# Moving the token sums, the first block sums' loads and the last tiles' roots in a one-core hybrid mixer layer

## The chip, the core and the metric

The kernel runs on one core of one Trainium2 chip. The metric is the device time of one execution in microseconds (us). "Span" is the time from the first to the last instruction of the one execution that the profiler recorded.

## What is computed

One layer: a normalised input goes through one projection, two head groups work on it (a gated recurrence and a gated convolution), and their concatenated result `mixed` (512 tokens x 2048) goes through the output projection, a root-mean-square norm and a residual addition. The part that the change touches is the end:

```python
mixed = jnp.concatenate([o_a, o_b], axis=-1)              # (1, 512, 2048)
y = jnp.einsum('btm,md->btd', mixed, w_out[l])            # 512 x 2048 by 2048 x 2048
x = x + y * lax.rsqrt(jnp.mean(y * y, axis=-1, keepdims=True) + EPS) * post_norm_g
```

## The kernel before, in words

All weights stream through a ring of `RING = 4` slots. A unit is 128 x 1024 of float32: SyncE (SP) loads it into `w_raw`; ScalarE (ACT) rounds it into `w_hi`; the rest `w_lo = w_raw - w_hi` is made by GpSimd (POOL, `lo_unit`, L430) for all units up to the first two of the last stage, and by VectorE (DVE, `fast_rest`, L1241) after that. TensorE (PE) multiplies each unit in three products (hi by hi, hi by lo, lo by hi), 24 matmuls of 128 x 512 for a full unit, 12 for a unit of the fast kinds.

The 2048 output columns are done in four chunks of 512. **Chunk 0** is a plain product, the loop over `s` in `range(OUT_U)` (8 units; `out_products`). In the same loop every engine still carries the last head (head 7) along: `slot(H-1, s)` on PE, `late(H-1, s)` on ACT and DVE, and the last convolution tile `ln_tile(J-1, ...)`. Unit `s` on PE waits for `mlo_done, 2s + 2`: rows `2s` and `2s+1` of `h_lo`, made by DVE in `mix_lo(at)` (L1177) from what ACT rounded in `mix_hi(at)` (L724). `mix_lo(12)` and `(13)` stand in DVE's step 5, `(14)` in step 6, `(15)` in step 7. The last of them needs head 7's result: PE's `slot(7, 6)`, ACT's logarithm and exponential (L684, L686), DVE's L1145 and L1148, then `mix_hi(15)`.

**Chunks 1 to 3** are done by `STEPS`, a list written out by hand: P1 x4, C 0, P2 x4, P5 x4, P6 0, 1, C 1, P6 2, 3, P7 ..., P3 ..., P4 ..., and C 5 to 7 last. C steps are plain products for chunk 1 (24 matmuls). The P steps get a 2 x 2 block product out of seven block products; they need sums of weights (`bsum`, `sum_weights`) and sums of tokens (`sum_sides(n, at)`, L1200: `n` 0 to 3 for the four sums, `at` 0 to 2 for their parts, 128 x 1024, 128 x 512, 128 x 512, in place in `mix`). P5 reads sum 1, P6 sum 2, P7 sum 0, P3 sum 3. ACT's `side_rounded` waits for them (`m_summed`), DVE's `side_rest` (L1232) follows.

SP's queue: units `s` of chunk 0 through L312, and behind each of units 4 to 7 one load of a `bsum` block (L384), 512 KB each. The first of these waits for `lev_done, 4 * H` (head 7's scores are done, since `bsum` lies in the same memory) and `qdec_ready, H`. Then the units of `LOADS` follow, each when its slot is free.

At the end PE does C 5 to 7 token tile by token tile (`tt` 0 to 3) and signals `y_mm` after each. ACT squares each tile from PSUM (L733), and only after the four squares does it take the roots, tile by tile: logarithm (L827), exponential (L829). DVE per tile: the sum of the tile's four partial sums (L1322), the product with the gain (`take_y`, L1181), four multiply-adds with the residual (L1328). SP stores the tile (L404), the last one in four pieces.

```python
for tt in range(TT):                      # DVE, the end
    dve.wait_ge(y_sq, TT * (CHUNKS - 1) + tt + 1)
    V.tensor_reduce(rst[:, TT + tt:TT + tt + 1], ssq[:, tt * CHUNKS:(tt + 1) * CHUNKS], AX.X, ALU.add).then_inc(y_ssum, 1)
    take_y(1, tt, y1[:, tt * 512:(tt + 1) * 512], bank(tt))
    dve.wait_ge(y_rs, 2 * (tt + 1))
```

Of the kernel before, what the change touches and what calls it, by code (L numbers as in the profile page):

```python
# [27 lines left out]
def build_layer(nc, x, pre_norm_g, post_norm_g, w_in, lb_logits, hg_norm_g, dw_kernel, dw_bias,  # L28
                conv_ln_g, conv_ln_b, w_out, out):
    fp32, fp32r, i8 = mybir.dt.float32, mybir.dt.float32r, mybir.dt.int8  # L30
    ALU, ACT, AX = mybir.AluOpType, mybir.ActivationFunctionType, mybir.AxisListType
    ds = bass.ds
    P = 128
    _, T, D = x.shape
# [3 lines left out]
    H = W_A // P  # L38
# [3 lines left out]
    TT = T // P  # L42
    UW = HK * P
    RING = 4
    EPS, LB_FLOOR = 1e-6, 1e-30
# [10 lines left out]
    CHUNKS = D // 512  # L56
    OUT_U = (W_A + W_B) // (2 * P)
    N_FAST = N_OUT + OUT_U
    HU = OUT_U // 2
# [33 lines left out]
    SIDE = {step: i for i, step in enumerate([step for step in STEPS if step[0] in ("P5", "P6", "P7", "P3")])}  # L93
    SIDES = 3
    SUM_PARTS = ((0, 4), (4, 2), (6, 2))
    SUM_ORDER = [(0, 0), (0, 1), (0, 2), (1, 0), (2, 0), (3, 0), (1, 1), (2, 1), (3, 1), (1, 2), (2, 2), (3, 2)]
    M_SUM = {done: at + 1 for at, done in enumerate(SUM_ORDER)}
    JOINED = {"c11": 2, "u2": 4, "u4": 5, "c22": 7, "u3": 9, "c12": 11, "c21": 13}
    SUM_OF = {"P7": 0, "P5": 1, "P6": 2, "P3": 3}
# [33 lines left out]
    with ctx:  # L133
# [175 lines left out]
        @block.sync  # L309
        def _(sp):  # L310
            def load_unit(n, slot, src, width):
                sp.dma_start(w_raw[:, slot * UW:(slot + 1) * UW].rearrange("p (k c) -> p k c", c=width),  # L312
                             src.rearrange("(k p) c -> p k c", p=P)).then_inc(raw_in[slot], 16)

            def in_unit(n, slot, half, col):
                load_unit(n, slot, w_in[0, half * UW:(half + 1) * UW, ds(col, P)], P)

            def first_loads():

                for at, n in enumerate(FIRST):  # L320
                    in_unit(n, n, n % 2, CONV_COLS[n // 2])
                    if at >= 2:
                        x_load(at)
                par_loads()

            def conv_loads(j):
                for s in range(CONV_U):
                    n = CONV_U * j + s
                    if n < RING:
                        continue  # L330
                    sp.wait_ge(raw_in[n % RING], 16 * (n // RING))
                    sp.wait_ge(lo_done, FIRST.index(n - RING) + 1 if n < 2 * RING else n - RING + 1)
                    if s < 4:
                        in_unit(n, n % RING, s % 2, CONV_COLS[s // 2] + j * P)
                    else:
                        k = VK * (2 * (j % VH) + s - 4)
                        load_unit(n, n % RING, w_in[0, k * P:(k + VK) * P, ds(COL_V + j // VH * VW, VW)], VW)

            def x_load(tt):
                if tt < 2:  # L340
                    for half in range(2):
                        a, b = half * UW, (half + 1) * UW
                        sp.dma_start(mix[:, tt * D + a:tt * D + b], x[0, tt * P:(tt + 1) * P, a:b]).then_inc(x_in[2 * tt + half], 16)
                else:
                    sp.dma_start(mix[:, tt * D:(tt + 1) * D], x[0, tt * P:(tt + 1) * P, :]).then_inc(x_in[2 + tt], 16)

            def par_loads():

                dwr = dw_kernel[0].rearrange("w (j c) -> (w j) c", c=P)
                R1 = TAPS * J - P  # L350
                sp.dma_start(stage[:, 0:P], dwr[0:P, :]).then_inc(par_in, 16)
                sp.dma_start(stage[0:R1, P:2 * P], dwr[P:TAPS * J, :]).then_inc(par_in, 16)
                sp.dma_start(stage[R1:R1 + J, P:2 * P], dw_bias[0].rearrange("(j c) -> j c", c=P)).then_inc(par_in, 16)
                for n, v in enumerate((conv_ln_g, conv_ln_b, lb_logits)):
                    sp.dma_start(stage[n * J:(n + 1) * J, 2 * P:3 * P], v[0].rearrange("(j c) -> j c", c=P)).then_inc(par_in, 16)
                sp.dma_start(stage[3 * J:3 * J + 1, 2 * P:3 * P], hg_norm_g).then_inc(par_in, 16)

            x_load(0)
            x_load(1)
            first_loads()  # L360
            for j in range(J):
                conv_loads(j)
            with sp.Fori(0, H) as h:
                for u in range(HEAD_U):
                    n = N_HEAD + HEAD_U * h + u
                    cut_before = held(sp, n - RING + 1)
                    sp.wait_ge(raw_in[u % RING], 16)
                    sp.wait_ge(lo_done, cut_before)
                    in_unit(n, u % RING, u % 2, HEAD_COLS[u // 2] + h * P)
            def out_rows(s):  # L370

                return slice(2 * P * PAIRS[s], 2 * P * (PAIRS[s] + 1))

            for s in range(OUT_U):
                n = N_OUT + s
                sp.wait_ge(raw_in[s % RING], 16 * (n // RING))
                sp.wait_ge(lo_done, n - RING + 1)
                load_unit(n, s % RING, w_out[0, out_rows(s), 0:512], 512)
                if s >= HU:
                    u = s - HU  # L380
                    if u == 0:
                        sp.wait_ge(lev_done, 4 * H)
                        sp.wait_ge(qdec_ready, H)
                    sp.dma_start(bsum[u].rearrange("p (k c) -> p k c", c=512),  # L384
                                 w_out[0, out_rows(u), ds(COL_2, 512)].rearrange("(k p) c -> p k c", p=P)).then_inc(first_in[u], 16)
            for q, step in enumerate(LOADS):
                n = N_FAST + q
                sp.wait_ge(raw_in[q % RING], 16 * (n // RING))
                if q < RING:
                    sp.wait_ge(lo_done, n - RING + 1)  # L390
                else:
                    used = LOADS[q - RING]
                    if used[0] in ("P1", "P6", "P4"):
                        sp.wait_ge(b_summed, SUMMED[used])
                    else:
                        sp.wait_ge(fast_lo, AT[used] - 1)
                s, col = load_of(step)
                load_unit(n, q % RING, w_out[0, out_rows(s), ds(col, 512)], 512)
            parts = 0
            for tt in range(TT):  # L400
                for a, b in out_parts(tt):
                    parts += 1
                    sp.wait_ge(y_out, parts)
                    sp.dma_start(out[0, tt * P:(tt + 1) * P, a:b], mix[:, tt * D + a:tt * D + b]).then_inc(stored, 16)  # L404
            sp.wait_ge(stored, 16 * parts)
# [68 lines left out]
        def _(act):  # L474
# [253 lines left out]
            def square(c, tt, y):  # L728

                if squares[0]:  # L730
                    act.wait_ge(y_sq, squares[0])
                squares[0] += 1
                A(near[:, 0:512], y, ACT.Square, accum_out=ssq[:, tt * CHUNKS + c:tt * CHUNKS + c + 1]).then_inc(y_sq, 1)  # L733

            def out_hi(s):
                n = N_OUT + s + AHEAD
# [82 lines left out]
            act.wait_ge(joined, JOINED["c21"])  # L819
            for tt in (0, 1):  # L820
                square(2, 2 + tt, pair_c21[:, tt * 512:(tt + 1) * 512])
            for tt in range(TT):
                act.wait_ge(y_mm, TT - 1 + tt + 1)
                square(1, tt, bank(tt))
            for tt in range(TT):
                act.wait_ge(y_ssum, tt + 1)
                A(rst[:, tt:tt + 1], rst[:, TT + tt:TT + tt + 1], ACT.Ln, scale=1.0 / D, bias=EPSB).then_inc(y_rs, 1)  # L827
                act.wait_ge(y_rs, 2 * tt + 1)
                A(rst[:, tt:tt + 1], rst[:, tt:tt + 1], ACT.Exp, scale=-0.5).then_inc(y_rs, 1)  # L829


        @block.vector
        def _(dve):
# [428 lines left out]
            for s in range(OUT_U):  # L1262
# [5 lines left out]
                    ln_tile(J - 1, s - 2, False)  # L1268
                for at in {2: (6, 7), 3: (8, 9), 4: (10, 11), 5: (12, 13), 6: (14,), 7: (15,)}.get(s, ()):
                    mix_lo(at)  # L1270
                if s == 4:
                    for at in range(3):
                        sum_sides(0, at)
                    for n in (1, 2, 3):
                        sum_sides(n, 0)
                if s == 6:
                    for n in (1, 2, 3):
                        sum_sides(n, 1)
            for m, (kind, u) in enumerate(STEPS):
                if m + 1 < len(STEPS) and STEPS[m + 1][0] in AHEAD_SUM:  # L1280
                    sum_weights(*STEPS[m + 1])
# [8 lines left out]
                if (kind, u) == ("P1", 3):  # L1290
                    dve.wait_ge(gain_in, 32)
                    for tt in range(TT):
                        dve.wait_ge(y_mm, tt + 1) if tt < TT - 1 else dve.wait_ge(unit_done, N_FAST)
                        take_y(0, tt, y0[:, tt * 512:(tt + 1) * 512], bank(tt))
                if (kind, u) == ("P2", 0):
                    for n in (1, 2, 3):
                        sum_sides(n, 2)
                if (kind, u) == ("P5", 2):
                    dve.wait_ge(kept, 1)
                    join(("P2", 3), pair_c11, 6, pair_c11)  # L1300
# [15 lines left out]
            join(("P4", 3), pair_c21, 4, pair_c21, JOINED["u3"])  # L1316
            gain(3, pair_c12, TT + 6)
            gain(2, pair_c21, TT + 8)
            dve.wait_ge(res_in, 16 * TT)
            for tt in range(TT):  # L1320
                dve.wait_ge(y_sq, TT * (CHUNKS - 1) + tt + 1)
                V.tensor_reduce(rst[:, TT + tt:TT + tt + 1], ssq[:, tt * CHUNKS:(tt + 1) * CHUNKS], AX.X, ALU.add).then_inc(y_ssum, 1)  # L1322
                take_y(1, tt, y1[:, tt * 512:(tt + 1) * 512], bank(tt))
                dve.wait_ge(y_rs, 2 * (tt + 1))
                dve.wait_ge(y_taken, TT * (CHUNKS - 1) + tt + 1)
# [321 lines left out]
```

## Time and profile before

| | us |
|---|---|
| median of 3 runs | 891.15 |
| lowest | 889.8 |
| the profiled execution, whole | 890.06 |
| its span | 888.2 |
| PE busy in the span | 858.7 (97%) |
| DVE busy | 648.5 (73%) |
| ACT busy | 413.8 (47%) |

Of the three timed runs one took 1669.31 us; the other two lie within 0.2% of each other. The whole time of the profiled execution is 1.86 us more than its span. TensorE's clock is given as a share of full speed (1.00 is 2.4 GHz, 0.50 is 1.2 GHz).

### The profile page before, as it was taken

How to read it: one execution, taken by the hardware profiler on the slowest of the kernel's cores; microseconds unless marked ns; L12 is line 12 of the kernel's file. 1: busy time of each engine (PE TensorE's matmuls, PEld its weight loads, DVE VectorE, ACT ScalarE, POOL GpSimd, SP SyncE). 2: the span in 40 equal slices, each digit the busy share in tenths (PEclk: the TensorE clock that was granted, in tenths of full speed). 3: DMA queues.
4: the chain of work that ended last, by engine and by line, in shares of the span. 5: the costliest groups of instructions: out<-in, count | busy, mean ns of one | idle time of the engine just before them, and what ended most of it. 6: DMA issues, size and time to landing. Idle time of an engine off the chain costs nothing.

```text
span 888.2 us, 12341 instructions
## 1 busy us (share of the span) xinstructions
PE 858.7 (97%) x4210; PEld 720.1 (81%) x4210; DVE 648.5 (73%) x1029; ACT 413.8 (47%) x648; POOL 311.9 (35%) x143
## 2 busy tenths in 40 slices
PE   8999999999999999999999999999999988999991
PEld 7988888888888888888888888888888866888881
DVE  4687778778778984948667594957759977697745
ACT  7523323322222464756457475646647641654331
POOL 3284444435434354242525334242533350000000
PEclk9999999999999999999999999999999998999996
DMA  9253333333333323232413313241321082434824
GB/s 308 79 147 100 102 101 96 96 95 95 94 96 95 95 71 104 63 96 58 125 53 94 94 47 94 71 118 47 94 94 48 1 308 74 140 119 142 296 84 189
DMA packets 119165, 96.07 MB, mean 108 GB/s; under 512 B 2864, under 2 KB 101465, under 8 KB 117849
## 3 DMA queue, kind: packets, MB, share of 16 engines
q1 hardware_dynamic: 118377, 90.33, 33.2%
q10 hardware_dynamic: 752, 5.25, 1.4%
q8 instruction: 23, 0.38, 0.2%
q14 instruction: 13, 0.11, 0.0%
HBM read 91.38 MB, written 4.19 MB: 108 GB/s over the span
## 4 chain that ended last, share of the span: by engine, by line
PE 94%; DVE 3%; issue 1%; DMA 1%; ACT 0%; DVEq 0%; POOL 0%; SPq 0%; ACTq 0%; POOLq 0%
PE banks L1425 19%; PE banks L1427 19%; PE banks L1426 19%; PE banks L1440 3%; PE banks L1442 3%; PE banks L1441 3%; PE banks L1598 3%; PE banks L1599 3%; PE banks L1597 3%; PE banks L1562 3%; PE banks L1371 3%; PE banks L1563 3%; PE banks L1564 3%; DVE mix L1200 1%; PE banks L1473 1%; PE banks L1483 1%
## 5 line engine op out<-in xcount | busy, mean ns | idle before, releaser
L430 POOL TENSOR_TENSOR w_lo<-w_raw,w_hi 128x1024 fp32r<-128x1024 f32 x122 | 305.8, 2510 | 420.3 <-ACT w_hi L485 419.8
L1425 PE MATMUL banks<-h_hi,w_hi 128*128 128x512 f32 x736 | 291.1, 396 | 0.0
L1427 PE MATMUL banks<-h_hi,w_lo 128*128 128x512 f32 x736 | 286.7, 390 | 0.0
L1426 PE MATMUL banks<-h_lo,w_hi 128*128 128x512 f32 x736 | 286.5, 389 | 0.0
L485 ACT ACTIVATE w_hi<-w_raw 128x1024 fp32r<-128x1024 f32 x120 | 126.5, 1055 | 175.7 <-PE banks L1427 81.3
L900 DVE SCALAR_TENSOR_TENSOR banks<-work,tap,banks 128x512 f32<-128x512 f32 x232 | 175.3, 756 | 8.0
L1427 PEld LDWEIGHTS banks<-h_hi,w_lo 128*128 128x128 f32 x736 | 138.1, 188 | 29.3
L1426 PEld LDWEIGHTS banks<-h_lo,w_hi 128*128 128x128 f32 x736 | 138.3, 188 | 28.2 <-issue 0.5
L1425 PEld LDWEIGHTS banks<-h_hi,w_hi 128*128 128x128 f32 x736 | 138.3, 188 | 27.9 <-issue 0.5
L1562 PE MATMUL banks<-w_hi,h_hi 128*128 128x512 f32 x128 | 51.3, 400 | 7.4 <-DVE h_lo L1177 7.4
L1563 PE MATMUL banks<-w_lo,h_hi 128*128 128x512 f32 x128 | 50.4, 394 | 0.0
L1564 PE MATMUL banks<-w_hi,h_lo 128*128 128x512 f32 x128 | 50.3, 393 | 0.0
L1440 PE MATMUL banks<-w_hi,h_hi 128*128 128x512 f32 x128 | 49.8, 389 | 0.0
L1441 PE MATMUL banks<-w_lo,h_hi 128*128 128x512 f32 x128 | 49.8, 389 | 0.0
L1442 PE MATMUL banks<-w_hi,h_lo 128*128 128x512 f32 x128 | 49.8, 389 | 0.0
L1241 DVE TENSOR_TENSOR w_lo<-w_raw,w_hi 128x1024 fp32r<-128x1024 f32 x22 | 26.7, 1222 | 13.1 <-ACT w_hi L757 13.1
L1562 PEld LDWEIGHTS banks<-w_hi,h_hi 128*128 128x128 f32 x128 | 24.4, 191 | 13.2 <-issue 8.2
L757 ACT ACTIVATE w_hi<-w_raw 128x1024 fp32r<-128x1024 f32 x24 | 24.9, 1054 | 21.4 <-PE banks L1564 10.7
L1101 DVE COPY_PREDICATED work<-mask,banks 128x192 f32<-128x192 int8 (+2 forms) x48 | 14.5, 303 | 27.5 <-PE banks L1483 20.2
L922 DVE SCALAR_TENSOR_TENSOR work<-banks,work 128x512 f32<-128x512 f32 x8 | 5.5, 692 | 32.1 <-ACT work L493 32.1
L1086 DVE COPY_PREDICATED work<-mask,banks 128x256 f32<-128x256 int8 x16 | 11.9, 743 | 23.3 <-PE banks L1473 22.5
L1564 PEld LDWEIGHTS banks<-w_hi,h_lo 128*128 128x128 f32 x128 | 24.4, 191 | 5.3
(211 smaller groups left out, 1261.6 us busy)
## 6 DMA issues: line engine op xcount, KB each, us to landing
w_raw<-in_w_in SPq DMA_DIRECT2D x112, 512.0 KB, 3.7
w_raw<-in_w_out SPq DMA_DIRECT2D x40, 512.0 KB, 4.5
mix<-in_x ACTq DMA_DIRECT2D x4, 1024.0 KB, 11.9
out_y<-mix SPq DMA_DIRECT2D x3, 1024.0 KB, 3.9
mix<-in_x SPq DMA_DIRECT2D x4, 512.0 KB, 5.5
mix<-in_x SPq DMA_DIRECT2D x2, 1024.0 KB, 10.0
work<-in_w_out SPq DMA_DIRECT2D x4, 512.0 KB, 8.7
gates<-in_post_norm_g ACTq DMA_DIRECT2D x1, 1024.0 KB, 6.7
```

The source lines that it names most:

```text
L430: g.tensor_tensor(w_lo[:, a], w_raw[:, a], w_hi[:, a].bitcast(fp32), ALU.subtract).then_inc(lo_done, 1)
L485: A(w_hi[:, a], w_raw[:, a], ACT.Copy).then_inc(hi_done, 1)
L900: V.scalar_tensor_tensor(dst, src, tp[:, w:w + 1], acc, ALU.mult, ALU.add).then_inc(tap_done, 1)
L1425: mm(bank(b), wh, hh, start=kt == 0, stop=False)
L1426: mm(bank(b), wh, hl, start=False, stop=False)
L1427: ins = mm(bank(b), wl, hh, start=False, stop=kt == KT - 1)
L1440: mm(o, h_hi[:, a], w_hi[:, w], start=vu == 0 and k == 0, stop=False)
L1441: mm(o, h_hi[:, a], w_lo[:, w], start=False, stop=False)
L1442: ins = mm(o, h_lo[:, a], w_hi[:, w], start=False, stop=vu == 2 * VH - 1 and k == VK - 1)
L1562: mm(o, h_hi[:, a], w_hi[:, w], start=first and k == 0, stop=False)
L1563: mm(o, h_hi[:, a], w_lo[:, w], start=False, stop=False)
L1564: ins = mm(o, h_lo[:, a], w_hi[:, w], start=False, stop=last and k == 1)
```

## The change

Four edits. The order of the sums (`SUM_ORDER`) becomes sum by sum, and their calls leave DVE's loop over `s` (steps 4 and 6) for the loop over `STEPS`: sums 0 and 1 stand in P2 0 and P2 1, sum 2 in P2 3, sum 3 in P5 1. The four `bsum` loads leave SP's loop over `s`, and each now stands behind one of the first four loads of `LOADS`; the wait for head 7's scores stands behind the first of these. On ACT, the root of each last tile follows its own square. For that the three other chunks' partial sums are added by DVE ahead of the tiles and scaled (eight instructions on one column each), and the logarithm takes them as its bias.

```diff
-    SUM_ORDER = [(0, 0), (0, 1), (0, 2), (1, 0), (2, 0), (3, 0), (1, 1), (2, 1), (3, 1), (1, 2), (2, 2), (3, 2)]
+    SUM_ORDER = [(n, at) for n in range(4) for at in range(3)]
...
                 load_unit(n, s % RING, w_out[0, out_rows(s), 0:512], 512)
-                if s >= HU:
-                    u = s - HU
-                    if u == 0:
-                        sp.wait_ge(lev_done, 4 * H)
-                        sp.wait_ge(qdec_ready, H)
-                    sp.dma_start(bsum[u].rearrange("p (k c) -> p k c", c=512),
-                                 w_out[0, out_rows(u), ds(COL_2, 512)].rearrange("(k p) c -> p k c", p=P)).then_inc(first_in[u], 16)
...
                 load_unit(n, q % RING, w_out[0, out_rows(s), ds(col, 512)], 512)
+                if q == 0:
+                    sp.wait_ge(lev_done, 4 * H)
+                    sp.wait_ge(qdec_ready, H)
+                if q < HU:
+                    sp.dma_start(bsum[q].rearrange("p (k c) -> p k c", c=512),
+                                 w_out[0, out_rows(q), ds(COL_2, 512)].rearrange("(k p) c -> p k c", p=P)).then_inc(first_in[q], 16)
...
-                A(near[:, 0:512], y, ACT.Square, accum_out=ssq[:, tt * CHUNKS + c:tt * CHUNKS + c + 1]).then_inc(y_sq, 1)
+                A(near[:, 0:512], y, ACT.Square, accum_out=ssq[:, tt * CHUNKS + (c - 1) % CHUNKS:tt * CHUNKS + (c - 1) % CHUNKS + 1]).then_inc(y_sq, 1)
...
+            act.wait_ge(y_ssum, 2 * TT)
             for tt in range(TT):
                 act.wait_ge(y_mm, TT - 1 + tt + 1)
                 square(1, tt, bank(tt))
-            for tt in range(TT):
-                act.wait_ge(y_ssum, tt + 1)
-                A(rst[:, tt:tt + 1], rst[:, TT + tt:TT + tt + 1], ACT.Ln, scale=1.0 / D, bias=EPSB).then_inc(y_rs, 1)
+                act.wait_ge(y_sq, squares[0])
+                A(rst[:, tt:tt + 1], ssq[:, tt * CHUNKS:tt * CHUNKS + 1], ACT.Ln, scale=1.0 / D,
+                  bias=rst[:, TT + tt:TT + tt + 1]).then_inc(y_rs, 1)
                 act.wait_ge(y_rs, 2 * tt + 1)
                 A(rst[:, tt:tt + 1], rst[:, tt:tt + 1], ACT.Exp, scale=-0.5).then_inc(y_rs, 1)
...
-                if s == 4:
-                    for at in range(3):
-                        sum_sides(0, at)
-                    for n in (1, 2, 3):
-                        sum_sides(n, 0)
-                if s == 6:
-                    for n in (1, 2, 3):
-                        sum_sides(n, 1)
...
-                if (kind, u) == ("P2", 0):
-                    for n in (1, 2, 3):
-                        sum_sides(n, 2)
+                if kind == "P2" and u < 2:
+                    for at in range(3):
+                        sum_sides(u, at)
+                if kind == "P2" and u == 3:
+                    for at in range(3):
+                        sum_sides(2, at)
+                if (kind, u) == ("P5", 1):
+                    for at in range(3):
+                        sum_sides(3, at)
...
             gain(2, pair_c21, TT + 8)
+            for tt in range(TT):
+                a = slice(TT + tt, TT + tt + 1)
+                V.tensor_reduce(rst[:, a], ssq[:, tt * CHUNKS + 1:(tt + 1) * CHUNKS], AX.X, ALU.add).then_inc(y_ssum, 1)
+            dve.wait_ge(y_ssum, TT)
+            for tt in range(TT):
+                a = slice(TT + tt, TT + tt + 1)
+                V.tensor_scalar(rst[:, a], rst[:, a], 1.0 / D, EPS, ALU.mult, ALU.add).then_inc(y_ssum, 1)
             dve.wait_ge(res_in, 16 * TT)
             for tt in range(TT):
                 dve.wait_ge(y_sq, TT * (CHUNKS - 1) + tt + 1)
-                V.tensor_reduce(rst[:, TT + tt:TT + tt + 1], ssq[:, tt * CHUNKS:(tt + 1) * CHUNKS], AX.X, ALU.add).then_inc(y_ssum, 1)
                 take_y(1, tt, y1[:, tt * 512:(tt + 1) * 512], bank(tt))
```

## Rows read from the trace of the kernel before

**Rows 1.** The page, part 1: busy us (share of the span), instructions.

```profile
PE 858.7 (97%) x4210; PEld 720.1 (81%) x4210; DVE 648.5 (73%) x1029; ACT 413.8 (47%) x648; POOL 311.9 (35%) x143
```

**Rows 2.** Waits of PE from 690 us on: in total, times, longest.

```profile
PE banks L1562 <- DVE h_lo L1177: 7.4, 1, 7.4
```

**Rows 3.** Windows: stretch, length, busy us of each engine, PE's granted clock, DMA, GB/s.

```profile
729.70:733.00 3.30, 0.00 (x0) 0.00 (x0) 3.20 (x2) 1.46 (x3) 3.29 (x2) 1.00 0.42 158
737.00:740.40 3.40, 3.33 (x8) 2.69 (x9) 3.15 (x6) 0.00 (x0) 0.00 (x0) 0.50 0.00 0
...
749.60:760.50 10.90, 10.90 (x50) 9.01 (x49) 7.28 (x9) 6.67 (x12) 0.00 (x0) 1.00 0.29 93
760.50:777.00 16.50, 16.50 (x74) 13.69 (x73) 10.80 (x12) 8.69 (x10) 0.00 (x0) 1.00 0.51 159
```

**Rows 4.** Chain that ended last, around the pause: start, us, what.

```profile
710.59 5.15 DMA w_raw<-in_w_out
...
716.72 0.62 ACT work L602
717.37 2.48 DVE mix L980
...
739.97 0.43 PE banks L1562
...
740.91 0.23 PE banks L1562
```

**Rows 5.** Timeline of DVE: start, us, line, operation, tiles, idle before it.

```profile
711.45 0.73 DVE L1138 SCALAR_TENSOR_TENSOR work<-work,ebl,banks 128x128 f32<-128x128 f32 x2
...
720.97 14.74 DVE L1200 TENSOR_TENSOR mix<-mix 128x1024 f32<-128x1024 f32 x6
...
740.36 0.75 DVE L1148 SCALAR_TENSOR_TENSOR mix<-work,par 128x512 f32<-128x512 f32 x1
```

**Rows 6.** Timeline of ACT.

```profile
728.90 1.06 ACT L757 ACTIVATE w_hi<-w_raw 128x1024 fp32r<-128x1024 f32 x1 [1.19 <-PE banks L1564]
...
730.57 0.63 ACT L686 ACTIVATE work<-work 128x512 f32<-128x512 f32 x1
```

**Rows 7.** Timeline of POOL.

```profile
724.70 8.61 POOL L430 TENSOR_TENSOR w_lo<-w_raw,w_hi 128x1024 fp32r<-128x1024 f32 x3 [0.27 <-ACT w_hi L485]
```

**Rows 8.** Waits of SP's queue from 650 us on.

```profile
SPq L384 <- PE banks L1492: 22.0, 1, 22.0
```

**Rows 9.** Groups of DVE by form, 718 to 770 us: busy, mean ns, idle before.

```profile
L1200 DVE TENSOR_TENSOR mix<-mix 128x512 f32<-128x512 f32 x8 | 9.8, 1238 | 0.4
L1200 DVE TENSOR_TENSOR mix<-mix 128x1024 f32<-128x1024 f32 x4 | 9.0, 2251 | 0.2
L1241 DVE TENSOR_TENSOR w_lo<-w_raw,w_hi 128x1024 fp32r<-128x1024 f32 x7 | 8.4, 1223 | 8.5 <-ACT w_hi L757 8.5
...
L1177 DVE TENSOR_TENSOR h_lo<-mix,h_hi 128x512 fp32r<-128x512 f32 x6 | 3.9, 684 | 0.8 <-ACT h_hi L724 0.8
```

**Rows 10.** Timeline of ACT and DVE at the end.

```profile
865.46 0.60 ACT L733 ACTIVATE near<-banks 128x512 f32<-128x512 f32 x1 [3.39 <-PE banks L1564]
...
869.54 0.60 ACT L733 ACTIVATE near<-banks 128x512 f32<-128x512 f32 x1 [3.39 <-PE banks L1564]
...
870.13 0.28 ACT L827 ACTIVATE rst<-rst,epsb 128x1 f32<-128x1 f32 x1
870.44 0.20 ACT L829 ACTIVATE rst<-rst 128x1 f32<-128x1 f32 x1
870.68 0.75 DVE L1328 SCALAR_TENSOR_TENSOR mix<-gates,rst,mix 128x512 f32<-128x512 f32 x1 [11.83 <-ACT rst L829]
...
873.33 0.15 DVE L1322 TENSOR_REDUCE rst<-ssq 128x1 f32<-128x4 f32 x1
873.40 0.68 DVE L1181 TENSOR_TENSOR work<-banks,gates 128x512 f32<-128x512 f32 x1
...
881.87 2.07 DVE L1328 SCALAR_TENSOR_TENSOR mix<-work,rst,mix 128x512 f32<-128x512 f32 x3
```

## The prediction

> **What bounds the kernel now.** I read the page first, for the engine that holds the time: PE is busy in 97% of the span [rows 1]. So the question is where PE pauses and what stands behind its last matmul. From 690 us on, PE waits for another engine exactly once: 7.4 us in front of unit 6 of chunk 0 (L1562), for DVE's L1177, which is `mix_lo` [rows 2]. The windows put the pause at 729.7 to 737.1; at its end the granted clock is 0.50, the lower level of 1.2 GHz, and PE does 8 matmuls in 3.3 us there [rows 3]. The chain around the pause shows 0.43 us for one matmul in that stretch and 0.23 us once the clock is back [rows 4].
>
> Who is late? DVE's timeline has six token sums (L1200) from 720.97 to 735.71, and `mix_lo(12)` and `(13)` stand behind them in DVE's order [rows 5]. The chain shows the first cause: a load that lands at 715.7, then ACT's L602, then DVE's L980 [rows 4]. DVE's head work before it ended at 712.2 [rows 5]; it then had nothing to do until L602, which stood on ACT behind `out_hi(3)`, the rounding of unit 5. That unit's load stood in SP's queue behind the first `bsum` load, which waited 22.0 us for head 7's scores [rows 8]. So both moved parts of the change bear on this one pause.
>
> The end is the second place. The last matmul ends near 869.5; ACT squares tile 3 and only then takes the first root, so DVE, which could work on tile 0 much earlier, sat idle 11.83 us and does four tiles in a row from 870.68 to 883.94 [rows 10]. Output stores take the rest up to 888.2, 4.26 us.
>
> **Part 1: sums and loads moved, the pause.** Unit 5's load no longer waits, so ACT rounds it on time and L602 runs before 712 (DVE gave it its input before the row at 711.45 [rows 5]), L980 at 712.2, right behind DVE's head work. Even at L980's price in the chain, 2.48 us [rows 4], it ends at 714.7. `mix_lo(13)` needs `mix_hi(13)`, which stands on ACT behind the rounding of unit 7, which needs the slot of unit 3 (716 on PE: 729.7 less units 4 and 5 at 5.44 and 2.5 us of head work between them); two such steps at 1.06 [rows 6] and about 0.6 put `mix_lo(12)` to `(14)` at 721 at the latest, also when POOL disturbs them. PE wants them at 729.7. The 7.4 us go.
>
> What is late next is unit 7, which wants `mix_lo(15)` at 729.66 + 24 x 0.227 = 735.1. PE's `slot(7, 6)` ends at 729.7 as before; ACT rounds unit F1 at 728.90 and its exponential L686 ends at 731.20, both as before [rows 6]. Then DVE's L1145 and L1148 (0.68 by L1177's form [rows 9], 0.75 [rows 5]), ACT's `mix_hi(15)` (0.63, by L686's form) and `mix_lo(15)` (0.68) come to 734.2 with the hand-overs between them. In the kernel before DVE came to L1148 only at 740.36. The margin is 0.9 us.
>
> POOL is the doubt here: it makes F1's rest from about 730.0 on, and L1148 and `mix_lo(15)` have two SBUF inputs each. In the kernel before, POOL's three operations up to 733.3 took 8.61 us [rows 7], 2.87 each. The Trainium skill (SBUF — State Buffer, Who interferes with whom) says that a DVE operation with two SBUF inputs and a GpSimd operation that reads SBUF exclude each other for a whole instruction, and that other such pairs don't touch. By that rule L1148 would wait to 732.4 and the margin would be 0.5, not 0.9.
>
> Without a pause the clock has no reason in this trace to fall (it is 1.00 in the windows beside the pause [rows 3]): 8 matmuls at 0.23 are 1.8 us instead of 3.4, so 1.6 more. Part 1: 7.4 + 1.6 = **9.0 us**. From below it could be less by what `mix_lo(15)` is late: bounded by L980's excess, 2.48 - 0.68 = 1.8 us, less the margin, so a loss of 0.9.
>
> **Part 1, the other side: where the work goes.** All twelve sums are 9.8 + 9.0 = 18.8 us in the kernel before [rows 9], 4.7 for one group of three. An undisturbed operation of the same shape takes 1.22 (128 x 1024, L1241) and 0.68 (128 x 512, L1177) [rows 9]; a group is 2.6. The nearer row is the clean one: POOL's last operation ends at 733.3 [rows 7], and the first moved sum runs after 750. The rule above says the same; by the disturbed row a group would be 4.7. I take 2.6 and keep 4.7 as the upper end.
>
> Does DVE have the room? In 749.6 to 777.0 it is idle 3.6 + 5.7 = 9.3 us with one group of 2.3 us already there [rows 3]. Four groups are 10.4, so 8.1 more: tight. I walk it through, with all PE times 9.0 earlier (P1 0 at 740.6, a P step 2.72 us, a C step 5.44). C 0 starts at 751.5, P2 0 at 756.9, P2 1 at 759.6, P2 2 at 762.4, P2 3 at 765.1, P5 0 at 767.8, P5 1 at 770.5, P6 0 at 778.7. ACT rounds a step when the unit four before it is done. DVE: rest of C 0 until 750.3 (1.1 ahead, as the kernel before has it), of P2 0 until 751.5; sum 0 until 754.1; rest of P2 1 until 755.3; sum 1 until 757.9; rest of P2 2 until 759.1 (3.3 ahead); of P2 3 until 760.3; sum 2 until 762.9; P5 0's two rests until 764.8 (3.0 ahead); P5 1's until 766.7 (3.8 ahead); sum 3 until 769.3; P5 2 until 771.2 (2.0 ahead); the join of c11 and P6 0's weight sum until 773.7; P5 3 until 775.6 (0.3 to 0.4 ahead); P6 0 with the next weight sum until 778.7, just in time. The sums of 512 overlap a little (three took 2.28 in the kernel before), which gives some 0.25 a group, 1 us in all, as a cushion. I take **0**, with 0 to 2 us at the clean price. ACT's `side_rounded` for P5 0 waits for sum 1's first part at 756.5; behind it in ACT's queue is the rounding of P5 0, which can't start before 759.6 anyway.
>
> The loads: units 5 to 7 and F0 go 15 us and more earlier; the four `bsum` loads are issued from 710.1 on, as before, with F1 to F3 between them, each when POOL has freed a slot (the last near 720). In the kernel before these took up to 11 us to land, with everything issued at once; even so the last is there by 731, and its sum (P1 3) is wanted at 743. Cost 0. The other users of SP's queue stand behind what frees their slots, which moves with PE.
>
> **Part 2: the roots.** Added on DVE: four reductions and four scalings of one column, 0.15 each by L1322 [rows 10]; the scaling is not in the trace, bounded by 0.07 (the distance at which L1181 follows L1322) and 0.28 (ACT's one-column L827). That is 0.6 to 1.7 us once, in front of tile 0. New wait: ACT's first square waits for them, and behind it stand the other squares. Tile 0's matmuls end near 857.3 in the kernel before (869.5 less three tiles), and the gains ahead of the additions about then; so tile 0's square is 0.6 to 1.7 late. Tiles come every 4.08 us (869.54 - 865.46), and DVE needs 0.68 + 0.75 + 2.07 = 3.5 for one [rows 10], so the lateness is gone by tile 2. ACT per tile: 0.60 + 0.19 + 0.28 + 0.20, 1.3.
>
> So tiles 0 to 2 are finished while PE works on the next. What is left behind the last square (870.13 in the kernel before): logarithm and exponential until 870.65, beside them `take_y` until 870.9, then 0.75 + 2.07 until 873.75. The same point was 883.94. **10.2 us** go: three tiles of 3.5 less 0.3 for the product that now stands in the path. The stores of the last tile's pieces end 4.26 us later, as before; with the third tile's megabyte only a little further ahead of them, 0 +/- 0.5.
>
> **Sum.** 9.0 + 10.2 = 19.2 us. Profiled execution: 890.06 - 19.2 = 870.9. The median of the runs shown is 1.1 higher, which would give 872.0; the lowest is 0.3 lower. I say 871.
>
> **Rivals.**
> *A, DVE becomes the bound in P2 to P6.* At the disturbed price (4.7 a group) the same walk puts P2 2's rest at 763.5 against 762.4, P5 0's 2.4 and P5 2's 3 us late, P6 0's some 6 to 7. Against it: nothing runs on POOL then. For it: my margin at P6 0 is nil. Time: 871 + 6.5 = 877.5. A milder form, 1 to 3 us in short pauses (or `mix_lo(15)` late by 0.9), gives 872 to 874.
> *B, the change lifts only half.* Something else than the sums holds `mix_lo(12)` and `(13)`, so the pause stays near 7 us and only the end is gained: 890.06 - 10.2 = 879.9. Against it: each link of the chain [rows 4] is either moved or has its input by 712.
> *C, slower.* The clock. PE runs through from 690 to 860 without the one rest it had; if the granted clock fell to the 0.50 that [rows 3] show for as little as 97 matmuls (19.2 / 0.20), 42 us of work at that level, all is given back (890), and beyond that point the kernel is slower: 911 at 200 matmuls. Against it: in this trace the level of 0.50 follows a pause and never full work.
>
> **Chances.** Both parts in full, 869 to 872.5: 0.66. Milder A, 872.5 to 875: 0.17. A in full: 0.08. B: 0.04. C: 0.01. Better than forecast, since the stores or later steps gain too: 0.04. The range that holds 8 in 10 runs from 868.5 to 876. A measurement of this kernel tells some 2% from no change; that line lies at 873.3 (from 891.15), or 872.3 from the profiled execution, only 1.4 to 2.4 us above the forecast. Faster by over 2%: 0.70 of the cases lie under it, less 0.07 for that closeness, 0.63. Within 2%: 0.36. Slower: 0.01.
>
> **What the profile will show.** Right: no wait of PE from 690 us to its last matmul, clock 1.00 through 729 to 745, first P1 matmul near 740.6; twelve L1200 after 750 at 1.2 and 0.7 us; the last matmul near 860.5; ACT alternating square, logarithm, exponential every 4.08 us; 7.9 us from the end of the last square to the end of the span, where it was 18.1. Wrong: PE waiting for L1241 or L1232 in P5 or P6 steps (A); PE waiting for L1177 near 729 or 735 (B, or POOL's port); DVE waiting for a `bsum` load; clock 0.50 anywhere in the stage (C).

## The result, and the profile after

The changed kernel takes 870.25 us (median of four runs, 869.83 to 870.59); the kernel before takes 890.71 beside it (median of four). The ratio is 0.9773, with a 95% interval of 0.9754 to 0.9793. One of these four, 1669.31 us, fell out of line: the ratio leaves it out, and the median of the other three is 890.27. The span is 868.4 us instead of 888.2, 19.8 less; I had forecast 19.2. The changed kernel's line numbers differ a little: `mix_lo` is L1176 (was L1177), the sums L1199 (L1200), the rests L1240 (L1241), the last multiply-adds L1331 (L1328), the matmuls of chunk 0 L1565 to L1567.

The page of the changed kernel, part 1, against [rows 1]:

```profile
PE 857.1 (99%) x4210; PEld 719.2 (83%) x4210; DVE 645.6 (74%) x1033; ACT 413.4 (48%) x648; POOL 311.2 (36%) x143
```

PE's work is the same to within 2 us, its share went from 97% to 99%: what was saved was PE's idle time. PE waits for no other engine between 690 us and its last matmul, where [rows 2] had 7.4 us. The windows of the changed kernel over the old pause, to be held against the first two of [rows 3]:

```profile
729.70:733.00 3.30, 3.30 (x16) 2.67 (x15) 1.50 (x2) 1.70 (x3) 2.42 (x1) 1.00 0.00 0
733.00:740.40 7.40, 7.40 (x34) 6.15 (x33) 5.47 (x6) 1.69 (x2) 0.00 (x0) 1.00 0.39 120
```

PE is busy for all of both, 34 matmuls stand where there were 8 in the last 3.4 us, and the clock is 1.00. DVE's timeline of the changed kernel shows the head's last work, against [rows 5]:

```profile
709.75 5.68 DVE L1176 TENSOR_TENSOR h_lo<-mix,h_hi 128x512 fp32r<-128x512 f32 x2
...
716.72 0.69 DVE L979 TENSOR_TENSOR mix<-work 128x512 f32<-128x512 f32 x1
717.32 5.30 DVE L1176 TENSOR_TENSOR h_lo<-mix,h_hi 128x512 fp32r<-128x512 f32 x5
731.47 0.69 DVE L1144 TENSOR_TENSOR work<-banks,work 128x512 f32<-128x512 f32 x1 [8.85 <-ACT work L685]
732.20 1.04 DVE L1147 SCALAR_TENSOR_TENSOR mix<-work,par 128x512 f32<-128x512 f32 x1
734.00 0.69 DVE L1176 TENSOR_TENSOR h_lo<-mix,h_hi 128x512 fp32r<-128x512 f32 x1 [0.76 <-ACT h_hi L723]
```

`mix_lo(10)` to `(14)` are done at 722.6, 7 us ahead of PE, where the kernel before had its six sums. Between `mix_lo(14)` and head 7's L1144 DVE has 8.85 us with nothing to do. `mix_lo(15)` is done at 734.7.

The moved sums, in the groups of DVE between 748 and 775 us by form, against [rows 9]:

```profile
L1199 DVE TENSOR_TENSOR mix<-mix 128x512 f32<-128x512 f32 x8 | 5.1, 684 | 0.0
...
L1199 DVE TENSOR_TENSOR mix<-mix 128x1024 f32<-128x1024 f32 x4 | 4.9, 1220 | 0.0
```

The same twelve operations took 18.8 us and now take 10.0. The end, in the timeline of ACT and of DVE, against [rows 10]:

```profile
856.49 0.60 ACT L732 ACTIVATE near<-banks 128x512 f32<-128x512 f32 x1 [2.83 <-PE banks L1567]
...
860.57 0.60 ACT L732 ACTIVATE near<-banks 128x512 f32<-128x512 f32 x1 [2.83 <-PE banks L1567]
861.06 0.20 ACT L732 ACTIVATION_READ_ACCUMULATOR near<-banks 128x1 f32 x1
861.29 0.29 ACT L826 ACTIVATE rst<-ssq,rst 128x1 f32<-128x1 f32 x1
861.61 0.20 ACT L829 ACTIVATE rst<-rst 128x1 f32<-128x1 f32 x1
```

```profile
848.29 0.34 DVE L1318 TENSOR_REDUCE rst<-ssq 128x1 f32<-128x3 f32 x4
848.67 0.34 DVE L1322 TENSOR_SCALAR rst<-rst 128x1 f32<-128x1 f32 x4
...
858.67 2.07 DVE L1331 SCALAR_TENSOR_TENSOR mix<-work,rst,mix 128x512 f32<-128x512 f32 x3
861.29 0.69 DVE L1180 TENSOR_TENSOR work<-banks,gates 128x512 f32<-128x512 f32 x1 [0.55 <-ACT near L732]
862.08 0.75 DVE L1331 SCALAR_TENSOR_TENSOR mix<-gates,rst,mix 128x512 f32<-128x512 f32 x1
862.75 2.07 DVE L1331 SCALAR_TENSOR_TENSOR mix<-work,rst,mix 128x512 f32<-128x512 f32 x3
```

DVE ends tile 2 at 860.74 and only tile 3 is left: 1.5 us from the start of its square to the first multiply-add, 2.7 us of multiply-adds, and 3.6 us from their end (864.82) to the end of the span. From the end of the last square to the end of the span it is now 7.2 us.

### The profile page after: what moved, and what is told of

Same layout as the page of the kernel before. It is cut to its first block, busy times and chain, and to the rows that moved or that the text cites. A ratio compares the mean times of both kernels' runs of the same rounds, so it can differ in the third digit from the quotient of the medians.

```text
span 868.4 us, 12345 instructions
## 1 busy us (share of the span) xinstructions
PE 857.1 (99%) x4210; PEld 719.2 (83%) x4210; DVE 645.6 (74%) x1033; ACT 413.4 (48%) x648; POOL 311.2 (36%) x143
## 4 chain that ended last, share of the span: by engine, by line
PE 98%; DVE 0%; ACT 0%; issue 0%; POOL 0%; DVEq 0%; ACTq 0%; POOLq 0%
PE banks L1428 19%; PE banks L1430 19%; PE banks L1429 19%; PE banks L1567 3%; PE banks L1565 3%; PE banks L1443 3%; PE banks L1566 3%; PE banks L1445 3%; PE banks L1444 3%; PE banks L1602 3%; PE banks L1600 3%; PE banks L1601 3%; PE banks L1374 3%; PE banks L1476 1%; PE banks L1486 1%; PE banks L1345 1%
## 5 line engine op out<-in xcount | busy, mean ns | idle before, releaser
L1565 PE MATMUL banks<-w_hi,h_hi 128*128 128x512 f32 x128 | 50.8, 397 | 0.0
L1567 PE MATMUL banks<-w_hi,h_lo 128*128 128x512 f32 x128 | 49.9, 390 | 0.0
L1240 DVE TENSOR_TENSOR w_lo<-w_raw,w_hi 128x1024 fp32r<-128x1024 f32 x22 | 26.8, 1220 | 9.6 <-ACT w_hi L756 9.5
L1566 PEld LDWEIGHTS banks<-w_lo,h_hi 128*128 128x128 f32 x128 | 24.0, 188 | 5.1 <-issue 0.2
L1565 PEld LDWEIGHTS banks<-w_hi,h_hi 128*128 128x128 f32 x128 | 24.0, 188 | 5.1 <-issue 0.2
```

What stands on the lines that cost most here:

```text
L1565: mm(o, h_hi[:, a], w_hi[:, w], start=first and k == 0, stop=False)
L1566: mm(o, h_hi[:, a], w_lo[:, w], start=False, stop=False)
L1567: ins = mm(o, h_lo[:, a], w_hi[:, w], start=False, stop=last and k == 1)
```

## The experiments

### The two halves, and the two parts of the first half

Four kernels put single edits back. `e1_sums_loads` has the sums and the loads moved and the end as before; `e2_sums_only` the sums alone; `e3_loads_only` the loads alone; `e4_end_only` only the roots and the advance sums. Each is the diff of the change with the other hunks left out; the core of `e2_sums_only` is:

```diff
 # against the kernel before; SP's loop, ACT and the end untouched
-    SUM_ORDER = [(0, 0), (0, 1), (0, 2), (1, 0), (2, 0), (3, 0), (1, 1), (2, 1), (3, 1), (1, 2), (2, 2), (3, 2)]
+    SUM_ORDER = [(n, at) for n in range(4) for at in range(3)]
...
-                if s == 4:
-                    for at in range(3):
-                        sum_sides(0, at)
-                    for n in (1, 2, 3):
-                        sum_sides(n, 0)
-                if s == 6:
-                    for n in (1, 2, 3):
-                        sum_sides(n, 1)
...
+                if kind == "P2" and u < 2:
+                    for at in range(3):
+                        sum_sides(u, at)
...
```

> The changed kernel with the end as it was before: sums and loads moved, roots after all four squares. My theory (the pause is worth 9.0 us and the two parts of the change add up): 890.3 - 9.0 = 881.3 by the fast level of the kernel before, no wait of PE after 690 us. Rival (the two parts share something, such as the granted clock or the stores): clearly off 881.3, by 2 us or more.

> Only the token sums are moved; the block sums' loads and the end are as before. My prediction held that both moved parts bear on the pause, and left open whether both are needed. Theory 1 (the sums alone suffice): L980 still comes late (near 717 to 720), but mix_lo(12) to (14) then follow by 727, before PE wants them at 729.7: 881.3, no pause. Theory 2 (the loads are needed too, since GpSimd is then still busy with units 7, F0 and F1 from 724.7 on and holds mix_lo up): a pause of 1 to 4 us is left, 882.5 to 886.

> Only the loads are moved; the six sums still stand in DVE's step 4, three in step 6. Theory 1 (an earlier start is enough): the sums run from about 718 with GpSimd busy for only two operations meanwhile, take some 7 to 10 us and not 14.7, and mix_lo(13) is there near 729: pause 0 to 1 us, 881 to 883. Theory 2 (six sums ahead of mix_lo are the cause, whenever they start): mix_lo(13) comes at 733 or later, pause 3 us or more, 885 to 888.

> Only the end is changed (each last tile's root behind its own square, the other chunks' partial sums ahead of the tiles). My theory: 10.2 us, whatever stands before it: 890.3 - 10.2 = 880.1, with the pause of 7.4 us unchanged. Rival (the end gains less by itself, its stores or roots wait for something that the other edits move): 882 or more.

| kernel | median us | ratio to before | waits of PE from 690 us, us |
|---|---|---|---|
| sums and loads | 880.5 | 0.9881 [0.9851, 0.991] | 0 |
| sums alone | 880.69 | 0.9873 [0.9847, 0.9898] | 0 |
| loads alone | 885.7 | 0.9933 [0.9911, 0.9955] | 2.6 |
| end alone | 880.34 | 0.9873 [0.9844, 0.9903] | 7.6 |

By the spans of the profiled executions (888.2 before) the first half gives 9.7 us by itself (878.5), the second 9.6 (878.6), and both together 19.8: they add up, and so do the ratios within their intervals (0.9881 x 0.9873 = 0.9755). With the end alone the pause stands as it was, 7.6 us. The 9.6 is a little low for a reason that lies outside the end: in that execution the clock stayed down longer after the pause (last section). From the start of PE's last matmul to the end of the span it is 19.1 us before, 8.3 with the end alone and 8.3 in the changed kernel, so the end is worth 10.8. Theory 1 holds for the sums: moved alone they remove the whole pause, and on top of them the loads add nothing that the time shows. Without the early loads L980 does come late. DVE's timeline of `e2_sums_only`:

```profile
717.26 2.46 DVE L980 TENSOR_TENSOR mix<-work 128x512 f32<-128x512 f32 x1 [5.05 <-ACT work L602]
719.64 9.68 DVE L1177 TENSOR_TENSOR h_lo<-mix,h_hi 128x512 fp32r<-128x512 f32 x5
```

The fourth of these five by itself, `mix_lo(13)`:

```profile
723.63 2.89 DVE L1177 TENSOR_TENSOR h_lo<-mix,h_hi 128x512 fp32r<-128x512 f32 x1
```

L980 starts at 717.26 (717.37 in [rows 4]), and five `mix_lo` (10 to 14) take 9.68 us, for GpSimd works from 720.38 to 728.78. Unit 6 needs them up to the fourth, `mix_lo(13)`: it is done at 726.5, and PE wants it at 729.7, 3.2 us later. The fifth is done at 729.3, where I had expected 727, but only unit 7 wants it, at about 735. What the early loads give is more margin: `mix_lo(13)` is done at 722.0 in the changed kernel, `mix_lo(14)` at 722.6.

The loads alone were expected at 881 to 883 by the one theory and at 885 to 888 by the other; the time, 885.7, is the second's, though the sums did behave as the first said. DVE's timeline of `e3_loads_only`:

```profile
722.43 8.22 DVE L1199 TENSOR_TENSOR mix<-mix 128x1024 f32<-128x1024 f32 x6
730.57 1.89 DVE L1176 TENSOR_TENSOR h_lo<-mix,h_hi 128x512 fp32r<-128x512 f32 x3
732.38 4.49 DVE L1199 TENSOR_TENSOR mix<-mix 128x512 f32<-128x512 f32 x3
736.79 0.68 DVE L1144 TENSOR_TENSOR work<-banks,work 128x512 f32<-128x512 f32 x1
```

The six sums take 8.2 us, not 14.7, and unit 6 is only 0.45 us late. But the three sums of step 6 stand ahead of head 7's L1144, whose input from ACT was there at 733.1, and hold it to 736.8. PE's timeline of that kernel has both waits:

```profile
732.01 0.47 PE L1561 MATMUL banks<-w_hi,h_hi 128*128 128x512 f32 x1 [0.45 <-DVE h_lo L1176]
...
739.85 0.47 PE L1561 MATMUL banks<-w_hi,h_hi 128*128 128x512 f32 x1 [2.12 <-DVE h_lo L1176]
```

The second is unit 7. In the kernel before it hid behind the first. The clock fell after this pause too (0.50 in the window 742 to 744), so the price of the clock stayed, and what was gained, 5.4 us of median, is about the waits' difference, 7.4 - 2.6 = 4.8. The span of this profiled execution is only 2.7 us shorter (885.5), because it was already 1.9 us late at unit 6: head 7's last matmuls start at 730.54, in the kernel before at 728.64. Its clock had also been at 0.50 from 18 to 20 us, where the kernel before had 1.00. Without that the span shows 4.6.

### What the loads and the advance sums are worth in the changed kernel

`e5_no_loads` is the changed kernel with the loads' hunks undone. `e6_plain_roots` keeps the new order of squares and roots but adds the four partial sums per tile:

```diff
             for tt in range(TT):
                 act.wait_ge(y_mm, TT - 1 + tt + 1)
                 square(1, tt, bank(tt))
-                act.wait_ge(y_sq, squares[0])
-                A(rst[:, tt:tt + 1], ssq[:, tt * CHUNKS:tt * CHUNKS + 1], ACT.Ln, scale=1.0 / D,
-                  bias=rst[:, TT + tt:TT + tt + 1]).then_inc(y_rs, 1)
+                act.wait_ge(y_ssum, tt + 1)
+                A(rst[:, tt:tt + 1], rst[:, TT + tt:TT + tt + 1], ACT.Ln, scale=1.0 / D, bias=EPSB).then_inc(y_rs, 1)
```

with ACT's wait for the advance sums and DVE's two loops ahead of the tiles gone, the partial sums in their old columns, and `tensor_reduce` back in front of `take_y`. `e11_sums_and_plain_roots` is both together.

> The changed kernel with the block sums' loads put back behind the ordinary ones' old places (units 4 to 7 of chunk 0), sums and end as changed. Theory (the loads are worth nothing once the sums are out of the way, as in the run with the sums alone): 870 to 870.5, no wait of PE from 690 us on. Rival (the margin that the early loads give is used up in the changed kernel): a pause of 1 us or more, 872 or later.

> The changed kernel, but the partial sums are added per tile as before (one reduction of four columns behind each tile's square), and the logarithm waits for it. Theory (the order of squares and roots is the whole gain at the end, the advance sums only take one small step out of the last chain): the reduction (0.15) and its hand-over go into the last tile's chain, 0.1 to 0.3 us more from the last square to the end; about 870.5. Rival (without the advance sums ACT and DVE wait for each other at every tile and fall behind the 4.08 us of PE): 873 or more.

> Only what the earlier runs showed to matter: sums moved, each root behind its own square with the per-tile reduction, block sums' loads in their old place, no advance sums. Theory (nothing else in the change has a price): 870.0 to 870.4, as the changed kernel. Rival (the loads or the advance sums pay once both are missing): 871.5 or more.

They take 870.31, 870.05 and 870.09 us, with ratios to the kernel before of 0.9766, 0.9764 and 0.9776, each within 0.002 or 0.003: no difference from the changed kernel that can be measured. The end of `e6_plain_roots`, in its timeline:

```profile
860.33 0.20 ACT L732 ACTIVATION_READ_ACCUMULATOR near<-banks 128x1 f32 x1
860.55 0.16 DVE L1317 TENSOR_REDUCE rst<-ssq 128x1 f32<-128x4 f32 x1 [0.48 <-ACT near L732]
860.63 0.68 DVE L1178 TENSOR_TENSOR work<-banks,gates 128x512 f32<-128x512 f32 x1
860.75 0.29 ACT L825 ACTIVATE rst<-rst,epsb 128x1 f32<-128x1 f32 x1 [0.22 <-DVE rst L1317]
861.07 0.20 ACT L827 ACTIVATE rst<-rst 128x1 f32<-128x1 f32 x1
861.41 0.75 DVE L1323 SCALAR_TENSOR_TENSOR mix<-gates,rst,mix 128x512 f32<-128x512 f32 x1
```

From the accumulator's read to the first multiply-add it is 1.08 us, and 1.02 (861.06 to 862.08) in the changed kernel. The root's own chain is longer by the reduction, but it ends at 861.27, and `take_y` ends at 861.31: the reduction is hidden behind the product. My 0.1 to 0.3 was one term too many.

### How much room DVE has, and whether the place of the sums counts

`e7_dve_plus_one` and `e10_dve_plus_two` compute the rest of a weight unit once or twice more than needed in four steps, with the same result. `e9_sums_in_a_row` has all twelve sums ahead of P1 0.

```diff
                 dve.wait_ge(hi_done, N_FAST + m + 1)
+                if STEPS[m] in DOUBLED:            # P2 1, P2 2, P5 0, P5 2
+                    for _ in range(2):             # 1 in e7
+                        dups[0] += 1
+                        V.tensor_tensor(w_lo[:, a], src, w_hi[:, a].bitcast(fp32), ALU.subtract).then_inc(dup_done, 1)
+                        dve.wait_ge(dup_done, dups[0])
                 V.tensor_tensor(w_lo[:, a], src, w_hi[:, a].bitcast(fp32), ALU.subtract).then_inc(fast_lo, 1)
```

```diff
+            for n in range(4):
+                for at in range(3):
+                    sum_sides(n, at)
             for m, (kind, u) in enumerate(STEPS):
...
-                if kind == "P2" and u < 2:
-                    for at in range(3):
-                        sum_sides(u, at)
...
```

> The changed kernel with one extra DVE operation of 1.22 us (the rest of a weight unit is computed twice) in each of the steps P2 1, P2 2, P5 0 and P5 2, 5 us in all: what rival A of my prediction would cost DVE. By the walk in my prediction, where P5 3 and P6 0 had no room: 5 us or so late at P6 0, 875. By the changed kernel's trace, where each sum group took 2.3 us and P6 0's rest was done 2.3 us ahead: 2 to 3.5 us of waits, 872.5 to 874, the first at P5 2. If DVE's idle time as a whole (9.3 us of 27 before) counted: no change, 870.3.

The 5 us named there are less than rival A adds: four groups at 4.7 us in place of 2.6 are 8.4 us more. Rival A's dose lies between the two runs.

> As the run with one extra DVE operation, with two of them in each of P2 1, P2 2, P5 0 and P5 2, 10 us in all. One brought 2.0 us of waits in the trace. If DVE's room was used up there (2.9 us of 5 hidden), nearly all of the next 5 us shows: waits of 6.5 to 8 us, 877 to 879. If each step has room of its own that one operation left over: 2 to 4 us, 873 to 875. A clock drop would add 1.5.

> The changed kernel with all twelve sums in one row right behind mix_lo(15), ahead of step P1 0, instead of spread over P2 0 to P5 1. Theory (the place counts: spreading lets DVE's idle time take them): 9.4 us of sums from 734.7 on push P1 2's rest to 748 (wanted at 746), then the gains and squares of chunk 0 and C 0's rest to 757.5 (wanted at 751.5): 5 to 6 us of waits, 875.5 to 877, with a clock drop 1 or 2 more. Rival (any place behind the head's work will do): 870.3.

| kernel | median us (runs) | span, us | waits of PE from 690 us, us |
|---|---|---|---|
| changed | 870.25 | 868.4 | 0 |
| one operation more in four steps | 873.89 (872.64, 872.89, 874.89, 875.15) | 870.7 | 2.0 |
| two more | 877.97 (877.89 to 878.27) | 876.1 | 4.9 |
| sums in a row | 877.94 (876.77 to 878.42) | 874.9 | 4.7 |

Of 5 us of extra work 2.0 show in the waits and 2.3 in the span; the expectation that counted the changed trace's margins was right, and DVE's idle time taken as a whole was not a measure of room. With 10 us the total is as expected, 877 to 879, but partly by luck: the waits are 4.9 us, between the two theories (2 to 4, and 6.5 to 8), and the rest came from elsewhere. The windows of `e10_dve_plus_two` show what came on top:

```profile
766.00:770.00 4.00, 2.90 (x13) 2.06 (x11) 3.93 (x5) 1.07 (x1) 0.00 (x0) 1.00 0.47 163
770.00:774.00 4.00, 3.10 (x8) 2.44 (x9) 4.00 (x5) 0.00 (x0) 0.00 (x0) 0.64 0.02 4
774.00:778.00 4.00, 4.00 (x18) 3.15 (x16) 3.93 (x6) 1.58 (x2) 0.00 (x0) 0.94 0.00 0
```

DVE is busy for nearly all of each, and the clock is down in the second and for a moment in the third: 4 x 0.36 + 4 x 0.06 = 1.7 us lost. That makes 6.6 of the 7.7 us by which the span grew. The last 1.1 us lie at the edges of the four waits: by the starts of its matmuls, usually 0.23 us apart, PE stood still for 5.5 us and not 4.9, and after a wait it takes 0.33 us or more to the second start.

With the sums in a row PE waits twice. PE's timeline of `e9_sums_in_a_row`:

```profile
746.93 0.50 PE L1594 MATMUL banks<-w_hi,h_hi 128*128 128x512 f32 x1 [1.24 <-DVE w_lo L1240]
...
756.20 0.58 PE L1559 MATMUL banks<-w_hi,h_hi 128*128 128x512 f32 x1 [3.52 <-DVE w_lo L1240]
```

P1 2 is 1.2 us late and C 0 3.5 us, and the clock is 0.81 and 0.76 in the two windows of 4 us from 754 on, another 1.7 us. The waits, 4.7 us, are a little under the 5 to 6 expected. The twelve sums took 9.44 us in a row, no longer than when spread. So their place alone is worth 7.7 us of median here: DVE's room for them lies in the P2 and P5 steps, not ahead of P1.

### Smaller stores at the very end

`e8_end_pieces` computes and stores the last 512 columns of the last tile in two halves.

```diff
-            w = 512 if tt == TT - 1 else D
-            return [(a, a + w) for a in range(0, D, w)]
+            if tt < TT - 1:
+                return [(0, D)]
+            return [(0, 512), (512, 1024), (1024, 1536), (1536, 1792), (1792, 2048)]
...
```

> The changed kernel with the last quarter of the last tile computed and stored in two halves of 128 x 256 (128 KB each). Theory (the last store's time is mostly fixed, its size matters little): 0 to 0.3 us gained, 870.0 to 870.3. Rival (the last stores are limited by the bytes queued in front of them): 0.4 to 1 us gained; or a loss of 0.1 to 0.3, since two DVE operations of half the size take longer than one.

It takes 870.76 us, ratio 0.9772 [0.9754, 0.979] against 0.9773: nothing gained. DVE's last three multiply-adds became four and took 2.20 us in place of 2.07, and from their end to the end of the span it is 3.9 us, not less than the 3.6 before. Neither the rival's gain nor a loss clear of the noise is there.

## Why the prediction held

**The pause, 9.0 us.** Right in size and cause. The sums' hunk gives 9.2 us of span by itself (888.2 against 879.0); in the changed trace PE starts P1 0 at 740.66 where the prediction said 740.6, against 749.61 before. The split, 7.4 us of waiting and 1.6 of clock, is read from the trace before. The 1.6 holds for that execution: after the same pause in `e4_end_only` the clock cost 3.0.

Two steps on the way came later than forecast, and the large margin hid it. The prediction had L980 at 712.2 and `mix_lo(12)` to `(14)` at 721 "at the latest"; they came at 716.7 and 722.6, because GpSimd, started earlier by the moved loads, held up `mix_lo(8)` and `(9)` ahead of them (last section).

**"Both moved parts bear on this one pause."** True of the chain and misleading for the price. The late load and the six sums each delay `mix_lo(13)`, but removing the sums alone is enough, and removing the late load alone gives 5.4 us and leaves 2.6 us of waits. I had walked the chain with both edits in place and had not asked what each would do alone; with the sums alone `mix_lo(13)` is 3.2 us ahead of PE's need.

**`mix_lo(15)`, next late, margin 0.9.** It was done at 734.69, and PE started unit 7 at 735.22: 0.5. L1147 took 1.04 us and not 0.75, while GpSimd was busy until 732.7. That is what the rule on the shared port in the Trainium skill (SBUF — State Buffer, Who interferes with whom) gave, 0.5. The prediction's 732.4 needs 2.4 us for GpSimd's operation, which none of its rows shows (they have 2.87, disturbed); it took 2.42. The same rule stood behind the price of the moved sums, and the trace bears it out: 1.22 and 0.68 us each once GpSimd is done, 10.0 us in all against 18.8.

**The new place of the sums, cost 0.** Right; but my walk found P6 0 "just in time", which was too tight. A group takes 2.34 us from start to start and not 2.6, and operations of 1.22 follow each other at 1.14. P5 3's rest was done at 773.7, 2.3 us before PE wanted it, where I had 0.4. Rival A did not come because its premise did not: the sums ran at the undisturbed price. Its own price was not far off. 5 us more cost 3.6 us of median and 10 us more cost 7.7, so 8.4 would cost some 6.4 us (an estimate on the straight line between these two runs), where the prediction had 6.5.

**The loads, cost 0.** Right, and once the sums are moved their gain is 0 as well.

**The end, 10.2 us.** From the start of PE's last matmul to the end of the multiply-adds it was 14.8 us and is 4.7: the order of squares and roots gave 10.1. The advance sums made tile 0's square 0.7 us late, as forecast (0.6 to 1.7), and it was made up. The term that was a little off is the stores: 3.6 us from the last multiply-add to the end, not 4.26. That is 0.7 better, outside my "0 +/- 0.5", and makes up the 0.6 us by which the span is better than forecast. The last tile's four stores land after 3.2 us in the median, 3.7 before. Tile 2's megabyte is now ready 4.1 us ahead of the last piece, 3.5 before; whether this distance is the cause was only argued.

**Rivals B and C.** Nothing else held `mix_lo`; the clock stayed at 1.00 through 130 us of unbroken work.

## What to carry to other kernels

Before moving work off an engine that makes the critical one wait, walk the chain once for each edit alone: here two causes stood in one chain. Either one removed alone gained time, 10.4 us of median for the sums and 5.4 for the loads, but with the sums gone the loads were free to keep. An engine's idle time summed over a stage is no room; the room is, step by step, how far each result is ahead of who wants it, and an extra operation in four steps is a cheap way to measure it. At a kernel's end look for per-tile results that wait for a whole loop of other tiles on a helper engine; letting each tile's small steps follow its own input was worth as much as the whole pause.

## What I had not expected of the hardware

**GpSimd and DVE held each other up in turn.** `mix_lo(8)` and `(9)` take 1.29 us together when GpSimd is idle (709.54 in `e2_sums_only`) and 5.68 us in the changed kernel. One by one, with GpSimd's two operations of the same time:

```profile
709.22 2.86 POOL L429 TENSOR_TENSOR w_lo<-w_raw,w_hi 128x1024 fp32r<-128x1024 f32 x1 [8.51 <-ACT w_hi L484]
709.75 2.88 DVE L1176 TENSOR_TENSOR h_lo<-mix,h_hi 128x512 fp32r<-128x512 f32 x1
712.03 2.85 POOL L429 TENSOR_TENSOR w_lo<-w_raw,w_hi 128x1024 fp32r<-128x1024 f32 x1
712.55 2.88 DVE L1176 TENSOR_TENSOR h_lo<-mix,h_hi 128x512 fp32r<-128x512 f32 x1
```

Each of DVE's operations ends 0.55 us after one of GpSimd's, and each takes 2.88 us where 0.68 is usual. GpSimd's take 2.86 and 2.85 where one takes 2.40 while DVE has nothing to do (723.21 in the same trace), so it pays too. The early loads thus made DVE 4.6 us later at the head's state (L1137 at 716.07, its counterpart at 711.48 in `e2_sums_only`); it was hidden, since PE wanted the result only at 721.8.

**The clock after pauses.** It was at 0.50 after PE's pauses of 7.4 (before), 7.6 (end alone), 3.5 (sums in a row), 2.1 (loads alone, behind one of 0.45) and 2.0 us (two operations more, behind one of 0.8), and stayed at 1.00 through single waits of 1.2 us (sums in a row) and 1.0 us (two operations more, and the profiled execution of one operation more). What a fall costs did not follow the length of the pause. By the windows from PE's next matmul on it was 1.6 to 1.7 us after pauses of 7.4, 3.5, 2.1 and 2.0 us, but 3.0 us after the 7.6 us of `e4_end_only`, nearly the same pause as before:

```profile
739.00:741.00 2.00, 2.00 (x7) 1.52 (x6) 1.97 (x3) 0.00 (x0) 0.00 (x0) 0.50 0.00 0
741.00:743.00 2.00, 2.00 (x6) 1.61 (x5) 1.24 (x3) 0.63 (x1) 0.00 (x0) 0.50 0.00 0
```

In the kernel before, the second of these windows has:

```profile
741.00:743.00 2.00, 2.00 (x10) 1.67 (x9) 1.24 (x3) 0.63 (x1) 0.00 (x0) 1.00 0.00 0
```

So a pause that is shortened from 7.4 to 2.1 us can keep this part of its price whole, as in the kernel with the loads alone. Whether a wait of 1 us can bring a fall too is open: two of the four executions of `e7_dve_plus_one` took 2.2 us longer than the others, at a mean clock of 0.995 against 0.997 and 0.998, and of these two there is no trace.
